# Expert gathers of a two-layer decoder trunk: v rows follow their u rows by one head instead of by a pair of heads

## Chip, cores, metric

One core of one Trainium2 chip runs one launch of the kernel, all in float32. The metric is the device time in microseconds (us) of that launch. It is the median of three runs.

## What is computed

The reference is a decoder trunk of two layers over one sequence of 256 tokens with 1024 channels. Layer 0 mixes tokens with gated linear attention, layer 1 with a gated DeltaNet. Behind each mixer stands a PEER channel mixer, and this is where the change is made. Every token has 8 heads. Each head picks 16 of 16,384 experts by product keys, and an expert is one row of `u` and one row of `v`, each of 1024 floats (4 KB):

```python
def peer_ffn(h, wq, k1, k2, u, v):
    ...
    v1, i1 = lax.top_k(s1, PEER_TOPK)
    v2, i2 = lax.top_k(s2, PEER_TOPK)
    ...
    sc, pos = lax.top_k(cand, PEER_TOPK)
    idx = jnp.take_along_axis(cand_idx, pos, axis=-1)
    gate = jax.nn.softmax(sc, axis=-1).astype(h.dtype)
    ...
    def block(args):
        tb, ib, gb = args
        ue = jnp.take(u, ib, axis=0)
        act = gb * jax.nn.gelu(jnp.einsum('nd,nkd->nk', tb, ue))
        ve = jnp.take(v, ib, axis=0)
        return jnp.einsum('nk,nkd->nd', act, ve)
```

So for each of 256 tokens, 128 rows of u and 128 rows of v are fetched in each of two layers. The order is fixed by the data: a head's v rows can be fetched as soon as its indices are known, but they can be weighted only after all 16 dots of that head are done.

## The kernel before

The function `decoder` interleaves the PEER mixers with the rest of layer 1. It runs four stages w = 0 to 3: layer 0 on tokens 0 to 127, layer 0 on tokens 128 to 255, then layer 1 on the same two blocks. Next to stages 1 and 2 runs the DeltaNet mixer of token block 0 and of block 1 (I call it the mixer). It has a ramp of projections (`gdn_qkv`), a core of chunked products, the projections `gdn_z` and `gdn_w_out`, and the queries and scores of layer 1's experts (`peer_wq`). Stage w+1 of layer 1 can't choose experts before that. The mixer of block 1 starts from the residual that stage 1 writes (L1144 to L1148).

A stage has 128 u gathers and 128 v gathers. A gather is one indirect DMA that POOL (GpSimd) issues: 128 rows of 4 KB, one to each partition.

- **u gathers** (L2025) bring slot s of all 128 tokens into one of 8 buffers `ub`. DVE (VectorE) multiplies the buffer with h and sums it into one column of `dots` (L1163).
- **v gathers** (L2038) bring, for each of four groups of 32 tokens, rows of several tokens by several slots, so that PE (TensorE) can sum them in PSUM with a 128 x 32 matrix of weights `z` (L1652, 8 matmuls for a set of four gathers). They use 12 buffers (9 of `vb`, 3 of `mods`). In the last phase of a stage every second set goes into `ub`.

Before the change all this is done by pairs of heads, 32 slots at a time. A stage has five phases (`phase`): u of pair 0 alone; u of pair p with v of pair p-1, one after the other, three times; v of pair 3 alone. A v gather has four tokens by 32 slots, and a pair has 8 sets.

At the end of a pair comes a chain over four engines: the last dot (DVE), gelu (ACT, ScalarE, L1353), gate times dots and a spread by `mask4` (`weights`, L1116 and L1117), a transpose (PE, L1621), and the copy into `z` (ACT, L1360). The indices take a similar way: `routing` (DVE, L1028 to L1090), a transpose (L1631) and `slot_rows` (L1106 to L1109) into `idx4`, from which the v gathers read. `routing(k)` picks the experts of pair k; `idx_ready` tells POOL that its u gathers may start. The first v gather of stage 0 also waits for `cols_summed`, which PE gives after L1713, since `vb` holds partial sums until then.

Each engine's program is a set of generators (`experts`, `mixer`) whose pieces carry due times; `interleave` sorts the pieces by these. The order is thus fixed when the kernel is built, and an engine runs it strictly in order. Due times of the expert side come from `phase`, from `turned_in` and `routed_in` (which slot a routing or transpose stands behind) and from `ROUTE_AT`. `landings` works out which buffer each gather uses and whom POOL waits for. Two details matter: a u gather n waits for dot n-8 (or, behind a stage's end, for the v set that used the buffer), and the first v set that uses `ub` in the last phase waits for all dots of the stage.

The routings of stages 2 and 3 begin only when the scores are there. In the last phase of stages 1 and 2, DVE runs three of them (pairs 0, 1, 2 of the next stage) and only then the residual (L1144 to L1148) and the next stage's dots; pair 3 is routed from slot 42 of the next stage.

## Time and profile before

| | |
|---|---|
| runs of the kernel before, us | 1881.61, 1894.21, 1881.12 (median 1881.61) |
| profiled execution, us | 1885.82 |
| its span, first to last instruction, us | 1884.0 |
| PE, DVE, ACT, POOL busy, share of the span | 76%, 64%, 21%, 58% |
| bytes moved, mean rate | 703.24 MB, 373 GB/s |
| indirect gathers | 512 of u, 512 of v |
| dots L1163 | 512, mean 1.22 us |

The profile is of one execution. An engine's timeline gives the start of a piece, its length and, in brackets, how long the engine sat idle before it and what ended this. Stretches (windows) give busy time of each engine, the granted PE clock as a share of full speed, the DMA share and the rate in GB/s. Times are counted from the first instruction.

### The profile page before, as it was taken

Reading aid. Unit: us, or ns where it says so; the run is one execution under the profiler, and the core shown is the slowest. Engines: PE = TensorE matmul, PEld = TensorE weight load, DVE = VectorE, ACT = ScalarE, POOL = GpSimd, SP = SyncE. Lnnn points to the kernel's source line nnn. Section 1 sums busy time; section 2 is a strip of 40 time slices with the busy share of each in tenths; the row PEclk is TensorE's granted clock in tenths of the full one; section 3 lists DMA queues with packets and bytes.
Section 4 is the critical chain, followed back from the end, with each engine's and each line's share of the span. In section 5 each row is a group of like instructions: output and inputs, shape, how many; then the busy total and the mean of one; then the engine's idle time right before and its main releaser. Section 6 shows DMA issues by size and latency. Waiting matters only on the chain.

```text
span 1884.0 us, 20383 instructions
## 1 busy us (share of the span) xinstructions
PE 1440.3 (76%) x7476; PEld 868.7 (46%) x7476; DVE 1206.4 (64%) x2707; ACT 387.9 (21%) x910; POOL 1088.5 (58%) x1067
## 2 busy tenths in 40 slices
PE   6989896756668758979898777897988862767567
PEld 6744696200011647757665376776756620101011
DVE  6588468788881677576443967867733498754440
ACT  1202110000000561451202265163221120000000
POOL 0111047777777566666653557576665357777754
PEclk8989995787779879989998877998989885676789
DMA  9989289999999999999999999899999999999997
GB/s 367 371 337 354 100 324 318 410 409 409 406 374 401 359 408 345 347 410 402 363 414 412 376 378 408 297 365 410 355 401 415 409 346 395 409 409 409 409 399 298
DMA packets 173972, 703.24 MB, mean 373 GB/s; under 512 B 23456, under 2 KB 23840, under 8 KB 155824
## 3 DMA queue, kind: packets, MB, share of 16 engines
q0 software_dynamic: 152640, 574.69, 78.5%
q1 hardware_dynamic: 21232, 127.25, 16.9%
q8 instruction: 59, 0.97, 0.2%
q14 instruction: 41, 0.34, 0.0%
HBM read 700.82 MB, written 1.05 MB: 373 GB/s over the span
## 4 chain that ended last, share of the span: by engine, by line
POOL 25%; PE 20%; DMA 20%; DVE 12%; issue 10%; ACT 3%; POOLq 0%; DVEq 0%; ACTq 0%
POOL ub L2025 12%; DMA ub<-in_peer_u,idx 11%; POOL vb L2038 9%; DMA vb<-in_peer_v,idx 5%; DVE ub L1163 5%; PE PS L1652 4%; PE PS L1699 3%; POOL mods L2038 3%; PE PS L1942 2%; POOL ub L2038 2%; PE PS L1863 2%; DMA ub<-in_peer_v,idx 2%; PE PS L1858 1%; PE PS L1845 1%; DVE ring L1282 1%
## 5 line engine op out<-in xcount | busy, mean ns | idle before, releaser
L2025 POOL DMA_INDIRECT ub<-in_peer_u,idx x512 | 541.7, 1058 | 339.4 <-DVE dots L1163 158.2
L1163 DVE CUSTOM_DVE_ANT_0 ub<-ub,h 128x1024 f32<-128x1024 f32 x384 | 464.3, 1222 | 225.3 <-DMA ub<-in_peer_u,idx 223.4
L1652 PE MATMUL PS<-vb,z 128*32 128x512 f32 x1348 | 407.7, 751 | 125.3 <-DMA vb<-in_peer_v,idx 122.0
L2038 POOL DMA_INDIRECT vb<-in_peer_v,idx x337 | 352.4, 1046 | 127.7 <-issue 99.1
L1652 PEld LDWEIGHTS PS<-vb,z 128*32 128x32 f32 x1348 | 66.0, 122 | 368.6 <-DMA vb<-in_peer_v,idx 271.2
L1163 DVE CUSTOM_DVE_ANT_0 ub<-ub,PS 128x1024 f32<-128x1024 f32 x128 | 154.2, 1220 | 111.0 <-DMA ub<-in_peer_u,idx 111.0
L1652 PE MATMUL PS<-mods,z 128*32 128x512 f32 x444 | 144.3, 754 | 56.1 <-DMA mods<-in_peer_v,idx 56.1
L2038 POOL DMA_INDIRECT mods<-in_peer_v,idx x111 | 114.5, 1032 | 33.8 <-issue 33.8
L1768 PE MATMUL PS<-hT,ring 128*128 128x128 f32 x1024 | 125.4, 285 | 2.9 <-DMA ring<-in_gdn_qkv 2.9
L1768 PEld LDWEIGHTS PS<-hT,ring 128*128 128x128 f32 x1024 | 122.5, 201 | 10.3 <-issue 6.7
L2038 POOL DMA_INDIRECT ub<-in_peer_v,idx x64 | 60.0, 937 | 83.8 <-DVE dots L1163 57.2
L1652 PEld LDWEIGHTS PS<-mods,z 128*32 128x32 f32 x444 | 23.4, 123 | 142.8 <-DMA mods<-in_peer_v,idx 120.4
L424 POOL DMA_DIRECT2D two_slots<-in_ada_wide x24 | 12.9, 537 | 125.2 <-DVE vb L664 57.4
L1652 PE MATMUL PS<-ub,z 128*32 128x512 f32 x256 | 68.7, 626 | 11.6 <-DMA ub<-in_peer_v,idx 11.6
L1463 ACT ACTIVATE ring<-ring,taps 128x128 f32<-128x128 f32 x256 | 76.4, 387 | 0.3
L1353 ACT ACTIVATE dots<-dots 128x32 f32<-128x32 f32 x16 | 3.7, 229 | 316.8 <-DVE dots L1163 316.8
L1942 PE MATMUL PS<-ring,hT 128*128 128x256 f32 x256 | 61.0, 399 | 5.8 <-ACT z L1360 3.8
L1991 PEld LDWEIGHTS PS<-hT,ring 128*128 128x128 f32 x512 | 60.8, 199 | 7.2 <-issue 5.0
L1961 PE MATMUL PS<-ring 128*128 128x256 f32 x256 | 60.6, 397 | 4.6 <-DMA ring<-in_gdn_w_out 4.6
L1991 PE MATMUL PS<-hT,ring 128*128 128x128 f32 x512 | 62.4, 283 | 1.5 <-ACT z L1360 1.5
L1699 PE MATMUL PS<-hT,ring 128*128 128x256 f32 x256 | 58.0, 387 | 1.2 <-DVE zero L1121 1.2
L1942 PEld LDWEIGHTS PS<-ring,hT 128*128 128x128 f32 x256 | 50.2, 199 | 18.2 <-ACT z L1360 4.5
(351 smaller groups left out, 2194.6 us busy)
## 6 DMA issues: line engine op xcount, KB each, us to landing
ring<-in_gdn_qkv SPq DMA_DIRECT2D x32, 1024.0 KB, 8.6
two_slots<-in_ada_wide POOLq DMA_DIRECT2D x24, 1024.0 KB, 10.1
ring<-in_peer_wq SPq DMA_DIRECT2D x24, 1024.0 KB, 8.0
ring<-in_gdn_z SPq DMA_DIRECT2D x16, 1024.0 KB, 8.7
ring<-in_gdn_w_out SPq DMA_DIRECT2D x16, 1024.0 KB, 8.6
ring<-in_gla_w_in SPq DMA_DIRECT2D x6, 2048.0 KB, 12.0
mods<-in_ada_wide POOLq DMA_DIRECT2D x12, 1024.0 KB, 7.7
ring<-in_ada_w SPq DMA_DIRECT2D x4, 2048.0 KB, 11.6
```

What stands on the lines that cost most here:

```text
L1163: dve.tensor_tensor_reduce(out=ub[:, n % UB, :], in0=ub[:, n % UB, :], in1=by_token, scale=1.0, scalar=0.0, op0=ALU.mult, op1=ALU.add, acc ...
L1282: dve.tensor_tensor(dst[:, vs, :], dst[:, vs, :], core.ps(name, lv, gq), ALU.add).then_inc(emptied["D"].sem, 1)
L1463: last = act.activation(tapped_by[:, j, c, :], here[:, c, j:j + P], ACT.Copy, scale=taps[:, j, 16 * hf + 4 * un + c:16 * hf + 4 * un + c + 1])
L1652: last = pe.matmul(y[32 * j:32 * j + 32, e, :], z[:, j, 28 * b:28 * b + 32], rows[:, e * 512:(e + 1) * 512], start=False, stop=False, skip ...
L1699: last = pe.matmul(PS[:, 3 + b % 2, c * S:(c + 1) * S], w[:, k, c * P:(c + 1) * P], hT[:, k, :], start=(k == 0), stop=(k == KD - 1))
L1768: last = pe.matmul(PS[:, 3 + un, (2 * bb + c) * P:(2 * bb + c + 1) * P], w[:, k, c * P:(c + 1) * P], hTm[:, k, :], start=(k == 0), stop=(k ...
L1863: last = pe.matmul(ps[:, e, :], Y[:, v_, :], XT[:, v_, :], start=True, stop=True)
L1942: last = pe.matmul(ps, hTm[:, k, :], w[:, k, :], start=(k == 0), stop=(k == KD - 1))
L1961: last = pe.matmul(ps, oT[:, part * KD + k, :], w[:, k, :], start=(part == k == 0), stop=(part == 1 and k == KD - 1))
L1991: last = pe.matmul(PS[:, 3 + un % 2, (2 * bb + c) * P:(2 * bb + c + 1) * P], w[:, k, c * P:(c + 1) * P], hTm[:, k, :], start=(k == 0), sto ...
L2025: pool.indirect_dma_start(ub[:, n % UB, :], None, u_rows, off).then_inc(u_land[n % UB].sem, 16)
L2038: pool.indirect_dma_start(rows, None, v_rows, off).then_inc(land.sem, 16)
```

## The change

The lag between u and v becomes one head. A stage has nine phases: u of head 0 alone (16 slots), u of head p with v of head p-1 (seven times 16 pairs of gathers), v of head 7 alone. A v gather has eight tokens by 16 slots, a head has 4 sets, and `z` is half as large. Gelu, weights, transpose and the copy into `z` are made per head, 32 times instead of 16, on tiles of 16 columns (the spread tile stays 128 x 128, by `mask8`). Routing stays by pairs; its index tile is spread in two parts and turned by two transposes, and `slot_rows` becomes one reduction and one copy. The last phase has 16 v gathers instead of 32, and DVE routes two pairs there instead of three. Pair 2 of stages 2 and 3 is now routed from slot 12 on in the next stage, pair 3 from slot 40 on. The number of gathers, dots and v matmuls doesn't change.

```diff
-            def turned_in(w, p):
...
-            def routed_in(w, p):
...
+            def routed_in(w):
+
+                k = w * PAIRS
                 if w == 0:
-                    return [[(0, 3, 8), (1, 20, 24)], [(2, 20, 24)], [(4, 3, 8), (3, 20, 24)], [(5, 3, 8), (6, 20, 24)]][p]
...
+                    return [(1, 7), (2, 32), (4, 48), (3, 64), (5, 80), (6, 96), (7, 112)]
+                return [] if w == 1 else [(k + 2, 12), (k + 3, 40)]
...
-                return W_AT[w] + scale * (0, 60, 152, 244, 336)[p], scale * (60, 92, 92, 92, 46)[p]
+                return W_AT[w] + scale * (30 + 47 * (p - 1) if p else 0), scale * (30 if p == 0 else 23 if p == HEADS else 47)
...
-                        pairs = turned_idx.rearrange("p (n a) -> p n a", a=2)
-                        link(dve.tensor_copy(half4, pairs[:, :, 0]))
-                        link(dve.tensor_tensor(half4, half4, pairs[:, :, 1], ALU.add))
-                        quads = half4.rearrange("p (n a) -> p n a", a=2)
-                        dve.tensor_tensor(idx4[:, k % IDX4, :], quads[:, :, 0], quads[:, :, 1], ALU.add).then_inc(rows_ready.sem, 1)
...
+                        link(dve.tensor_reduce(rows_f[:], turned_idx.rearrange("p (n a) -> p n a", a=8), AX, ALU.add))
+                        dve.tensor_copy(idx4[:, k % IDX4, :], rows_f[:]).then_inc(rows_ready.sem, 1)
...
+                        link(dve.tensor_tensor(mine, dots[:, q % 2, :], mine, ALU.mult))
+                        dve.tensor_tensor(spread_a[:], mine.unsqueeze(1).to_broadcast([P, 8, TOPK]), mask8[:], ALU.mult).then_inc(acts_ready.sem, 1)
...
-                                        for n in range(3):
-                                            yield ROUTE_AT[w + 1] + 12 * n
-                                            for i, _ in enumerate(routing(k + n)):
-                                                yield ROUTE_AT[w + 1] + 12 * n + 0.75 * i + 1
+                                        for n in range(2):
+                                            yield ROUTE_AT[w + 1] + 18 * n
+                                            for i, _ in enumerate(routing((w + 1) * PAIRS + n)):
+                                                yield ROUTE_AT[w + 1] + 18 * n + i + 1
...
-                                                last = pe.matmul(y[32 * j:32 * j + 32, e, :], z[:, j, 28 * b:28 * b + 32],
...
+                                            last = pe.matmul(y[32 * j:32 * j + 32, e, :], z[:, j, 24 * b:24 * b + 32],
```

How the order moves is seen at three places. First POOL at the start of stage 0. Before:

```order
L2010 IOTA iota 128x16
L2025 DMA ub<-in_peer_u,idx 128x1024 x33
L2038 DMA vb<-in_peer_v,idx 128x1024
L2025 DMA ub<-in_peer_u,idx 128x1024
L2038 DMA vb<-in_peer_v,idx 128x1024
```

and after:

```order
L2012 IOTA iota 128x16
L2028 DMA ub<-in_peer_u,idx 128x1024 x17
L2043 DMA vb<-in_peer_v,idx 128x1024
L2028 DMA ub<-in_peer_u,idx 128x1024
L2043 DMA vb<-in_peer_v,idx 128x1024
```

The first v gather stands behind 17 u gathers instead of 33.

Second, PE in the ramp of stage 1: the last projections of the mixer (L1768, after: L1770) and the start of its core (L1795, after: L1797). L1621 (after: L1625) is the transpose of the weights, L1652 (after: L1657) a v set. Before:

```order
L1768 MATMUL PS<-hT,ring 128x128 x64
L1751 MATMUL PS<-ones,ring 128x1 x8
L1758 MATMUL PS<-ident,inv 128x128 x8
L1768 MATMUL PS<-hT,ring 128x128 x32
L1795 MATMUL PS<-tri,g 128x128 x4
L1621 MATMUL PS<-ident,spread_a 128x128
```

and after:

```order
L1625 MATMUL PS<-ident,spread_a 128x128
L1607 MATMUL PS<-ones,zero 128x512 x2
L1770 MATMUL PS<-hT,ring 128x128 x16
L1657 MATMUL PS<-vb,z 32x512 x8
L1770 MATMUL PS<-hT,ring 128x128 x16
L1753 MATMUL PS<-ones,ring 128x1 x8
L1760 MATMUL PS<-ident,inv 128x128 x8
L1770 MATMUL PS<-hT,ring 128x128 x16
L1657 MATMUL PS<-vb,z 32x512 x8
L1770 MATMUL PS<-hT,ring 128x128 x16
```

The first weights of the stage are now turned in the middle of the ramp, and v sets stand between its projections; before, none stood there.

Third, DVE in the ramp of stage 2 after the change. L1081 to L1087 are the three longest steps of `routing` for pair 2 of that stage, L1168 the dots, L1227 to L1231 the mixer:

```order
L1227 TENSOR_TENSOR ring<-ring 128x512
L1168 ISA ub,dots<-ub,h 128x1024
L1168 ISA dots 128x1
L1081 TENSOR_TENSOR fold<-cand,iota 128x1024
L1230 TENSOR_TENSOR ring<-ring 128x512
L1231 TENSOR_TENSOR ring<-ring 128x512
L1240 TENSOR_TENSOR be<-be,beta 128x16
L1168 ISA ub,dots<-ub,h 128x1024
L1168 ISA dots 128x1
L1085 TENSOR_TENSOR fold<-fold,topf 128x1024
L1168 ISA ub,dots<-ub,h 128x1024
L1168 ISA dots 128x1
```

The same place before had the dots and the mixer alone:

```order
L1214 TENSOR_TENSOR hT<-hT,PS 128x512
L1222 TENSOR_TENSOR ring<-ring 128x512
L1163 ISA ub,dots<-ub,h 128x1024
L1163 ISA dots 128x1
L1225 TENSOR_TENSOR ring<-ring 128x512
L1226 TENSOR_TENSOR ring<-ring 128x512
L1235 TENSOR_TENSOR be<-be,beta 128x16
L1163 ISA ub,dots<-ub,h 128x1024
L1163 ISA dots 128x1
```

A routing that stood behind the last dot of stage 1 now stands among the first dots of stage 2.

## Rows read from the trace of the kernel before

**Rows 1.** The page: span and rate.

```profile
span 1884.0 us, 20383 instructions
...
HBM read 700.82 MB, written 1.05 MB: 373 GB/s over the span
```

**Rows 2.** Stretches: PE, PEld, DVE, ACT, POOL busy, PEclk, DMA share, GB/s.

```profile
246.00:312.00 66.00, 61.48 (x324) 58.19 (x322) 49.12 (x130) 8.70 (x19) 40.21 (x33) 0.76 0.91 328
...
1060.00:1100.00 40.00, 30.88 (x149) 18.98 (x150) 34.11 (x101) 11.66 (x23) 22.77 (x20) 0.72 0.91 330
...
1540.00:1577.00 37.00, 0.90 (x2) 0.36 (x2) 36.38 (x76) 4.24 (x6) 24.47 (x26) 0.50 0.95 351
1584.00:1813.00 229.00, 150.24 (x361) 23.94 (x362) 126.57 (x254) 4.32 (x9) 172.87 (x185) 0.71 1.03 409
```

**Rows 3.** Timelines of PE, DVE and POOL at the start of stage 0.

```profile
276.59 16.97 PE L1713 MATMUL PS<-ones,vb 128*128 128x1 f32 x96
...
276.79 0.22 DVE L1106 COPY fold<-PS 128x64 f32<-128x64 f32 x1 [4.78 <-PE PS L1631]
...
312.31 1.09 POOL L2038 DMA_INDIRECT vb<-in_peer_v,idx  x1 [0.30 <-issue]
```

**Rows 4.** Issues of L2025 (u): 296 to 312, then 1540 to 1577.

```profile
L2025 POOL DMA_INDIRECT ub<-in_peer_u,idx x9: 933/1461/1988, 296.3 to 311.1; - x9
...
L2025 POOL DMA_INDIRECT ub<-in_peer_u,idx x26: 932/937/1836, 1539.2 to 1575.9; - x26
```

**Rows 5.** Timelines at the end of stage 1; 16th v gather of the last pair.

```profile
1018.17 1.23 DVE L1163 CUSTOM_DVE_ANT_0 ub<-ub,h 128x1024 f32<-128x1024 f32 x1 [4.42 <-DMA ub<-in_peer_u,idx]
...
1028.29 0.88 DVE L1028 MAX8 top<-mods 128x8 f32<-128x128 f32 x4 [8.06 <-ACT mods L1573]
...
L2038 POOL DMA_INDIRECT ub<-in_peer_v,idx x2: 937/938/940, 1032.1 to 1033.3; - x2
...
DMA to landing us min/median/max: 13.5/13.6/13.6
...
1066.68 0.94 POOL L2025 DMA_INDIRECT ub<-in_peer_u,idx  x1 [7.28 <-PE PS L1652]
...
1074.76 0.29 DVE L1090 TENSOR_TENSOR spread_i<-idxf,mask 128x128 f32<-128x128 f32 x1
...
1075.81 1.12 PE L1607 MATMUL PS<-ones,zero 128*128 128x512 f32 x2
...
1078.31 1.22 DVE L1163 CUSTOM_DVE_ANT_0 ub<-ub,h 128x1024 f32<-128x1024 f32 x1
```

**Rows 6.** The same at the end of stage 2.

```profile
L2038 POOL DMA_INDIRECT ub<-in_peer_v,idx x1: 938/938/938, 1500.6 to 1500.6; - x1
...
DMA to landing us min/median/max: 11.5/11.5/11.5
...
1525.08 0.93 POOL L2025 DMA_INDIRECT ub<-in_peer_u,idx  x1 [0.31 <-issue]
...
1542.79 1.21 DVE L1163 CUSTOM_DVE_ANT_0 ub<-ub,PS 128x1024 f32<-128x1024 f32 x1
...
1544.28 0.94 POOL L2025 DMA_INDIRECT ub<-in_peer_u,idx  x1 [2.89 <-DVE dots L1163]
1545.52 1.84 POOL L2025 DMA_INDIRECT ub<-in_peer_u,idx  x1 [0.30 <-DVE dots L1163]
```

**Rows 7.** Timelines of ACT and PE in the ramp of stage 1.

```profile
655.71 1.28 ACT L1469 ACT_TABLE_LOAD   x1
657.00 0.22 ACT L1469 ACTIVATE be<-gc 128x16 f32<-128x16 f32 x1
...
689.50 1.28 ACT L1353 ACT_TABLE_LOAD   x1
...
692.34 0.63 ACT L1440 ACTIVATE vT<-ring 128x512 f32<-128x512 f32 x1
...
692.56 0.47 PE L1621 MATMUL PS<-ident,spread_a 128*128 128x128 f32 x1 [7.84 <-DVE spread_a L1117]
```

More of the change, by code:

```diff
@@ L1149, in experts @@
                                     break
-                                ahead = [(routing(j), j, first) for j, first in routed_in(w, p)]
-                                late = {5: [k] if k == 0 else [k, k + 1], 12: [k + 2] if k else []} if w != 1 and p == 0 else {}
                                 if layer and p == 0:
@@ L1362, in experts @@
[L1362 to L1368 removed]
+                                    act.activation(z[:].rearrange("p j (b m) -> p j b m", m=4 * 8)[:, :, :, 0:8],
+                                                   turned_act.rearrange("p (j b a) -> p j b a", j=4, a=8), ACT.Copy).then_inc(z_made.sem, 1)
```

231 lines of the change are left out of this document (116 added, 115 removed).

## The prediction

> **What bounds the kernel now.** I read the page first: 700.82 MB are read in a span of 1884.0 us, 373 GB/s on average [rows 1]. Then the stretches. Where u and v gathers alternate and nothing else asks for the DMA, it runs at 409 GB/s for 229 us without a break [rows 2]. A gather is 128 x 4096 bytes = 524,288 bytes, so it takes 1.28 us there. At that rate the 700.82 MB would take 1713 us. The kernel is therefore bound by DMA, plus some 170 us in which the DMA runs below its rate. The change leaves every byte in place, so it can only move time in and out of those 170 us.
>
> The reader should look for them at the seams of the four stages: 328 GB/s in the first 66 us of stage 0, 330 GB/s between stages 1 and 2, 351 GB/s at the start of stage 3 [rows 2]. In the last two, DVE is busy for 34.1 of 40 us and 36.4 of 37 us: the seams belong to DVE. Last come the timelines around each seam [rows 3, 5 to 7]; they say which wait ends last.
>
> **The change, part by part.** The sum is made against the profiled execution, 1885.8 us, that is the span of 1884.0 us and 1.8 us around it. It lies 4.2 us above the median of the runs, 1881.6 us.
>
> *Steady phases.* Gathers, dots and v matmuls are the same in number and size. In the long stretch DVE is busy 126.6 of 229 us and PE 150.2 [rows 2]. The 16 added ends of a head (gelu, a weights step of 0.2 + 0.3 us like the spread of 0.29 us in [rows 5], a transpose, a copy into z) are about 1.3 us of work each, spread over four engines. They hide under the DMA. The chain also has time: a head's first v set lands four u and four v gathers behind the head's last dot, some 10 us by 1.28 us. Cost 0. If that cover were gone, 16 chains of about 5 us would be 80 us; nothing in the stretch points that way.
>
> *Start of stage 0.* One would hope that v gathers fill the 66 us at 328 GB/s, which lack (1 - 328/409) x 66 = 13 us. They can't do so early. The first v gather needs `cols_summed`, and PE gives it at 276.6 + 17.0 = 293.6 us [rows 3], behind projections that the change doesn't move. POOL runs in order. After the change it has issued 17 u gathers by about 280 (the last needs dot 8, which stands behind the index rows that DVE makes at 276.8), then stands until 293.6. From there u and v alternate at 1.28 us: the 34th gather goes out at 293.6 + 16 x 1.28 = 314. Before, the 33rd and 34th go out at 311.1 and 312.3 [rows 3, 4]. So the hoped-for gain is eaten by a wait that is late next: cost 1 to 2 us, I take +1, bounds -4 (POOL's issues are shorter, see below) and +5.
>
> *Ramp of stage 1.* Here two effects meet. Before, PE sits 7.8 us in front of the transpose of the first weights, and on ACT the gelu with its two table loads takes from 689.5 to 692.3, right on the way to the core [rows 7]. Both move into the middle of the ramp, where ACT and PE have pauses: a gain of up to 2.8 us. Against this, PE must now take three v sets before the core starts. The last of these twelve v gathers is the 40th gather of the stage, against some 34 before, and six gathers are 6 x 1.28 = 8 us of DMA; most of it is paid by two 1 MB weight blocks that are fetched later (2 x 2 x 1.28 = 5 us). Besides, the lists of instructions have 4 more table loads in stage 1 and 6 more in stage 2, at 1.28 us each: 5 and 8 us of ACT. ACT is idle for most of the span, so I charge a third to the path. Net for stage 1: -2.8 + 3 + 1.7 = +2, bounds -4 and +8. Of this I take +1.
>
> The row shows what a table load costs: it starts at 655.71, lasts 1.28 us, and the next activation starts at 657.00, 0.01 us behind it [rows 7]. The Trainium skill, ScalarE: Activation LUTs, section "What ACT_TABLE_LOAD costs", adds a drain of about 1.38 us to each load, 2.66 us in all. By that rule the ten loads would be 27 us of ACT instead of 13. The trace disagrees with the drain here.
>
> *Seam of stages 1 and 2.* This is the largest term. Before, the last dot ends at 1019.4, the scores arrive at 1028.3, and three routings run from 1028.3 to 1075.0, 15.6 us each; y closes at 1076.9, and the first dot of stage 2 starts at 1078.3 [rows 5]. So the three routings just fit under the 32 last v gathers. After the change only 16 v gathers are left when the last dot is done. The DMA is saturated, so the place in its queue decides: the last u row lands where before the 16th v gather of the last pair landed, at 1033.3 + 13.6 = 1046.9 [rows 5]. The last dot then ends at 1048.3 instead of 1019.4. Two routings of 15.8 us (each has one more spread of 0.29 us) and the weights step take DVE to 1048.3 + 0.8 + 31.6 = 1080.7. The residual takes 1078.3 - 1075.0 = 3.3 us. The first dot of stage 2 starts at 1084.0: +5.7 us. The new wait is y, closed at 1076.9, waiting for DVE. Behind it are queued the mixer of block 1, which reads the residual, and all dots, and behind the dots POOL, whose ninth u gather needs a dot. The u indices themselves are ready at 1049.1 + 15.8 = 1065, against an issue at 1066.7 [rows 5]; they just don't bind. Charge +5.5, bounds +1 (last dot earlier) and +11 (last dot at 1054, if the last 12 v gathers, which wait for it, end no earlier than now).
>
> *Ramp of stage 2.* The third routing, 15.5 us of DVE, moves in among the first 28 dots. In its favour, six fewer dots stand before the core, 7.4 us. Net 8 us more DVE work in about 75 us, in which DVE waits now and then. But DVE runs in order, and the 1.2 us steps stand between the mixer's own. I take half: +4, with the table loads and the effects of stage 1, bounds 0 and +10.
>
> *Seam of stages 2 and 3.* Same working. The 16th v gather of the last pair lands at 1500.6 + 11.5 = 1512.1 [rows 6]; the last dot ends at 1513.4, routings at 1545.8, residual at 1549.1, against a first dot at 1542.8: +6.3 us. Here the DMA decides alone. Nine dots at 1.24 us later, at 1560.2, POOL may issue the 17th u gather, and from then on v gathers fill in at 1.28 us: the 33rd gather goes out at 1560.2 + 16 x 1.28 = 1580.7. Before, the 32nd went out at 1575.9 [rows 4], the 33rd 1.24 us later at 1577.1. That is +3.5. Charge +3, bounds +1 and +7. The fourth routing is spread over slots 12 to 27: 1.1 us a step with a dot of 1.2 us, under 2.56 us for two gathers. No cost.
>
> *End.* 28 v gathers behind the last dot become 12, with the same last landing. Cost 0.
>
> **Sum.** 1 + 1 + 5.5 + 4 + 3 = 14.5 us. 1885.8 + 14.5 = 1900.3 against the profiled execution, and 1881.6 + 14.5 = 1896 against the median.
>
> **Rivals.**
>
> A, faster: the one-sided stretches are what starves the DMA, and the change halves them. The mechanism is POOL's issue time. In stage 0, while dots read `ub` and h from SBUF back to back, an issue of a u gather takes a median of 1.46 us and up to 1.99; in stage 3, where h lies in PSUM, it takes 0.94 [rows 4]. With the 0.3 us between issues, 1.76 us is more than the DMA's 1.28. When v gathers alternate, DVE works half as densely and the issues should shrink. The Trainium skill, SBUF — State Buffer, section on the two sides of SBUF, gives the cause: DVE and GpSimd share one port pair under an exclusive lock, and a DVE operation with two SBUF inputs takes it. By that rule the trace agrees in stages 0 and 3. The price: the three seams of [rows 2] lack 13 us, (1 - 330/409) x 40 = 8 us and (1 - 351/409) x 37 = 5 us, together 26 us. Half of it would give 1869, all of it 1856; I take 16 us, 1866. It decides if the first dot of stage 2 isn't later than about 1079. Against it stands that two of the three seams end in a wait for DVE, which grows.
>
> B, clearly slower: the head's chain doesn't hide in stages 1 and 2. PE waited 7.8 us for one such chain in the ramp [rows 7]. The eight added ones could cost PE 1 to 2 us each, and the v sets in the ramp hold the core back by their full 8 us: the sum plus 10 to 15 us, 1906 to 1911.
>
> C, nothing: routing two pairs instead of three cancels against the later last dot, because stages 1 and 2 are bound by the DMA in their second half and catch up. 1882, within 4 us. For it speaks that the DMA's queue is deep when the last dot ends, 13.5 us from issue to landing [rows 5]: there the DMA sets the pace.
>
> D, the change doesn't do what it says at the start: it is part of the sum, since v gathers don't start before 293.6.
>
> **How the numbers follow.** A measurement tells about 1% from no change, 18.8 us: 1862.8 and 1900.4. Chances: forecast 0.42, of which 0.31 within 1% and 0.11 beyond; A 0.22, its 16 us being just under 1%: 0.12 beyond, 0.10 within; B 0.22, all beyond; C 0.14, all within. Faster 0.12, same 0.55, slower 0.33. The bounds of the terms add up to -6 and +41; that all fall on one side is rare, so the forecast's own range is 1886 to 1908. The whole range reaches down to A's 1866 and up to B's 1911: 1865 to 1912.
>
> **What would show it.** Right: the first dot of stage 2 comes 5 to 6 us later measured from y's closing, with DVE busy and no idle before the residual; the first v gather is issued at 293.6 behind a wait for PE; the stretch of stage 3 stays at 409 GB/s. Wrong: DVE idle before the residual at both seams (then A or C), or idle time of PE in front of the transposes in stages 1 and 2 that sums to over 20 us (B).

## The result and the profile after

The changed kernel takes 1917.9 us (median of four runs, 1915.7 to 1921.9), the kernel before 1882.1 in the same comparison: a ratio of 1.0177 (95% interval 1.0149 to 1.0204). It is slower by 1.8%. The forecast was 1896 with a range up to 1912, so the result lies outside. The two profiled executions below differ by 30.1 of these 35.8 us. One remark on all runs: ratios and their intervals leave out executions in a slower state of the chip, the medians of the experiments don't, so the two can differ (most in run 11).

The page of the changed kernel, its span beside 1884.0 in [rows 1]:

```profile
span 1914.1 us, 20618 instructions
...
PE 1443.3 (75%) x7508; PEld 856.0 (45%) x7508; DVE 1215.1 (63%) x2739; ACT 420.9 (22%) x961; POOL 1078.3 (56%) x1067
```

Over the span as a whole no engine is near its limit, and the long stretch of stage 3 stays at 409 GB/s, as in [rows 2]. The time went into the other places. Stretches of the changed kernel, columns as in [rows 2]: the first 20 us in which v gathers could have helped, then stage 1 cut at the mixer's two cores (ramp, core 1, between them, core 2), then the rest:

```profile
280.00:300.00 20.00, 10.76 (x48) 10.16 (x49) 16.94 (x52) 2.17 (x4) 8.34 (x7) 0.50 0.37 114
...
624.10:703.10 79.00, 54.50 (x369) 43.76 (x369) 44.56 (x84) 45.25 (x114) 56.95 (x51) 0.81 0.99 386
703.10:775.20 72.10, 61.85 (x483) 51.79 (x483) 51.74 (x95) 21.61 (x54) 37.72 (x38) 0.95 0.94 343
775.20:834.90 59.70, 48.89 (x379) 38.00 (x379) 32.54 (x61) 32.49 (x93) 41.12 (x38) 0.92 1.00 396
834.90:908.80 73.90, 64.26 (x498) 52.98 (x499) 53.31 (x98) 22.84 (x56) 41.32 (x41) 0.95 0.97 365
...
1600.00:1840.00 240.00, 150.29 (x388) 24.05 (x388) 146.06 (x315) 8.33 (x17) 181.40 (x193) 0.74 1.03 409
```

The same of the kernel before (start, ramp, core 1, between, core 2):

```profile
280.00:300.00 20.00, 18.63 (x92) 18.54 (x91) 19.59 (x47) 1.51 (x2) 11.18 (x10) 0.51 0.76 230
...
620.00:683.70 63.70, 43.85 (x317) 42.70 (x318) 43.53 (x83) 37.37 (x91) 38.48 (x34) 0.79 0.99 382
683.70:766.10 82.40, 66.29 (x504) 52.47 (x502) 59.13 (x108) 28.56 (x74) 53.62 (x52) 0.94 0.96 365
766.10:820.40 54.30, 48.80 (x378) 38.66 (x378) 30.96 (x57) 31.45 (x85) 40.55 (x38) 0.94 0.94 367
820.40:896.10 75.70, 63.50 (x498) 51.54 (x497) 55.46 (x100) 21.56 (x58) 46.84 (x43) 0.93 1.02 404
```

The reader is to see two things. The ramp grew from 63.7 to 79.0 us, with DMA full in both: the core starts late because more gathers are served ahead of it. To serve them takes transfer time and also PE's own time. PE is busy in the ramp for 10.7 us more (54.5 for 43.9) and idle for 4.6 us more, and the matmuls of v sets, of which there were none before, are 9.3 us of it (the ramp, L1657 alone; PE and PEld busy, PEclk, DMA share, GB/s):

```profile
624.10:703.10 79.00, 9.29 (x48) 1.68 (x48) 0.81 0.99 386
```

The edits of phase 0 to the changed kernel below move the transfers and PE's work on them together, so their shares aren't told apart on this side. The second thing: DMA time lost, (1 - rate/409) x length, moved: core 1 loses 8.9 us before and 11.6 after, the piece between 5.6 and 1.9, core 2 0.9 and 8.0. With the other pieces of the stage the loss grows by 6.5 us, about the stage's extra length (6.8). The end of the mixer is hardly late: its last scores are out 434.6 us behind the stage's first dot, before 432.6 (stage 2: 442.0 and 439.6). What is late is the last dot, 433.7 us behind the first instead of 399.4.

Cut by y's closing and by the first dots, the two profiled executions differ by 30.1 us (all in us):

| part | before | after | difference |
|---|---|---|---|
| to the first u gather | 246.0 | 241.8 | -4.2 |
| stage 0, from there to y's closing | 372.7 | 380.9 | +8.2 |
| stage 1, first dot to y's closing | 456.9 | 463.7 | +6.8 |
| y's closing to first dot of stage 2 | 1.4 | 7.2 | +5.8 |
| stage 2 | 458.5 | 464.9 | +6.4 |
| y's closing to first dot of stage 3 | 6.0 | 14.0 | +8.0 |
| stage 3 | 333.7 | 332.8 | -0.9 |

(The seam between stages 0 and 1 has 1.4 in both.) The -4.2 is not the change's: over all profiles of this study the first u gather comes at 241 to 250 us, with either lag.

PE ahead of the two cores of stage 1, after the change (timeline; L1797 is the core's first piece):

```profile
664.71 0.47 PE L1625 MATMUL PS<-ident,spread_a 128*128 128x128 f32 x1 [9.65 <-DVE spread_a L1123]
...
694.72 1.04 PE L1657 MATMUL PS<-mods,z 128*32 128x512 f32 x2 [2.12 <-DMA mods<-in_peer_v,idx]
699.75 1.06 PE L1657 MATMUL PS<-mods,z 128*32 128x512 f32 x1 [3.99 <-DMA mods<-in_peer_v,idx]
703.14 1.05 PE L1797 MATMUL PS<-tri,g 128*128 128x128 f32 x7
...
834.01 0.47 PE L1625 MATMUL PS<-ident,spread_a 128*128 128x128 f32 x1 [5.41 <-DVE spread_a L1123]
```

Ahead of core 1 stand a head's transpose (9.65 us of waiting) and three v sets; right ahead of core 2 stands another head's transpose (5.41). None of the three v sets stood there before. Over the whole kernel PE's wait for `spread_a` went from 63.0 us in 10 pieces to this (waits):

```profile
PE PS L1625 <- DVE spread_a L1123: 97.8, 27, 16.8
```

In stages 1 and 2 alone it more than doubled (waits from 620 to 1543 us before, then from 624 to 1574 after):

```profile
PE PS L1621 <- DVE spread_a L1117: 17.9, 4, 7.8
```

```profile
PE PS L1625 <- DVE spread_a L1123: 40.4, 13, 9.6
```

The seam of stages 1 and 2, DVE after the change (timeline), to be held against [rows 5]:

```profile
1056.56 1.23 DVE L1168 CUSTOM_DVE_ANT_0 ub<-ub,h 128x1024 f32<-128x1024 f32 x1 [1.50 <-DMA ub<-in_peer_u,idx]
...
1075.82 0.19 DVE L1091 TENSOR_TENSOR idx<-cand 128x32 uint32<-128x32 f32 x1
...
1091.51 0.19 DVE L1091 TENSOR_TENSOR idx<-cand 128x32 uint32<-128x32 f32 x1
...
1092.25 0.68 DVE L1151 TENSOR_TENSOR h<-PS,h 128x512 f32<-128x512 f32 x1
...
1094.91 1.22 DVE L1168 CUSTOM_DVE_ANT_0 ub<-ub,h 128x1024 f32<-128x1024 f32 x1
```

y closed at 1087.7 (PE, L1610). The residual carries no wait in brackets: it comes straight behind the second routing. And POOL at the start of stage 0 (timeline), against [rows 3, 4]:

```profile
275.66 0.94 POOL L2028 DMA_INDIRECT ub<-in_peer_u,idx  x1 [10.90 <-DVE dots L1168]
289.83 0.94 POOL L2043 DMA_INDIRECT vb<-in_peer_v,idx  x1 [13.24 <-PE PS L1715]
291.07 1.62 POOL L2028 DMA_INDIRECT ub<-in_peer_u,idx  x1 [0.30 <-issue]
292.99 1.87 POOL L2043 DMA_INDIRECT vb<-in_peer_v,idx  x1 [0.30 <-issue]
```

### The profile page after: what moved, and what is told of

It is laid out like the page before. It is cut to its first block, busy times and chain, and to the rows that moved or that the text cites. A ratio compares the mean times of both kernels' runs of the same rounds, so it can differ in the third digit from the quotient of the medians.

```text
span 1914.1 us, 20618 instructions
## 1 busy us (share of the span) xinstructions
PE 1443.3 (75%) x7508; PEld 856.0 (45%) x7508; DVE 1215.1 (63%) x2739; ACT 420.9 (22%) x961; POOL 1078.3 (56%) x1067
## 4 chain that ended last, share of the span: by engine, by line
POOL 26%; PE 22%; DMA 15%; DVE 12%; issue 11%; ACT 3%; POOLq 0%; ACTq 0%; DVEq 0%
POOL ub L2028 13%; POOL vb L2043 9%; DMA ub<-in_peer_u,idx 9%; DVE ub L1168 4%; PE PS L1657 4%; POOL mods L2043 3%; DMA mods<-in_peer_v,idx 3%; PE PS L1701 3%; PE PS L1993 2%; PE PS L1847 1%; PE PS L1865 1%; PE PS L1860 1%; DVE ring L1287 1%; DMA ring<-in_peer_wq 1%; DMA ring<-in_gdn_z 1%
## 5 line engine op out<-in xcount | busy, mean ns | idle before, releaser
L1168 DVE CUSTOM_DVE_ANT_0 ub<-ub,h 128x1024 f32<-128x1024 f32 x384 | 465.2, 1222 | 266.2 <-DMA ub<-in_peer_u,idx 264.3
L1657 PE MATMUL PS<-vb,z 128*32 128x512 f32 x1440 | 433.8, 761 | 134.0 <-DMA vb<-in_peer_v,idx 121.1
L2043 POOL DMA_INDIRECT vb<-in_peer_v,idx x360 | 369.8, 1027 | 155.2 <-issue 107.0
L1657 PEld LDWEIGHTS PS<-vb,z 128*32 128x32 f32 x1440 | 68.4, 122 | 382.7 <-DMA vb<-in_peer_v,idx 268.5
L1657 PE MATMUL PS<-mods,z 128*32 128x512 f32 x480 | 170.0, 772 | 77.6 <-DMA mods<-in_peer_v,idx 77.6
L1168 DVE CUSTOM_DVE_ANT_0 ub<-ub,PS 128x1024 f32<-128x1024 f32 x128 | 155.4, 1220 | 114.0 <-DMA ub<-in_peer_u,idx 113.7
L2043 POOL DMA_INDIRECT mods<-in_peer_v,idx x120 | 120.3, 1003 | 36.6 <-issue 36.6
L1770 PEld LDWEIGHTS PS<-hT,ring 128*128 128x128 f32 x1024 | 124.8, 203 | 10.6 <-issue 8.8
L1770 PE MATMUL PS<-hT,ring 128*128 128x128 f32 x1024 | 127.2, 287 | 1.4 <-DMA ring<-in_gdn_qkv 1.4
L1657 PEld LDWEIGHTS PS<-mods,z 128*32 128x32 f32 x480 | 27.0, 123 | 182.1 <-DMA mods<-in_peer_v,idx 154.5
L1358 ACT ACTIVATE dots<-dots 128x16 f32<-128x16 f32 x32 | 6.9, 216 | 456.8 <-DVE dots L1168 456.2
L1625 PE MATMUL PS<-ident,spread_a 128*128 128x128 f32 x32 | 12.4, 387 | 97.8 <-DVE spread_a L1123 97.8
L1625 PEld LDWEIGHTS PS<-ident,spread_a 128*128 128x128 f32 x32 | 5.0, 158 | 128.2 <-DVE spread_a L1123 124.9
L1287 DVE TENSOR_TENSOR ring<-ring,PS 128x512 f32<-128x512 f32 x72 | 46.5, 683 | 22.0 <-PE PS L1865 22.0
L2043 POOL DMA_INDIRECT ub<-in_peer_v,idx x32 | 30.2, 945 | 48.4 <-DVE dots L1168 39.6
## 6 DMA issues: line engine op xcount, KB each, us to landing
ring<-in_gla_w_in SPq DMA_DIRECT2D x6, 2048.0 KB, 10.8
```

The source lines that it names most:

```text
L1168: dve.tensor_tensor_reduce(out=ub[:, n % UB, :], in0=ub[:, n % UB, :], in1=by_token, scale=1.0, scalar=0.0, op0=ALU.mult, op1=ALU.add, acc ...
L1287: dve.tensor_tensor(dst[:, vs, :], dst[:, vs, :], core.ps(name, lv, gq), ALU.add).then_inc(emptied["D"].sem, 1)
L1657: last = pe.matmul(y[32 * j:32 * j + 32, e, :], z[:, j, 24 * b:24 * b + 32], rows[:, e * 512:(e + 1) * 512], start=False, stop=False, skip ...
L1770: last = pe.matmul(PS[:, 3 + un, (2 * bb + c) * P:(2 * bb + c + 1) * P], w[:, k, c * P:(c + 1) * P], hTm[:, k, :], start=(k == 0), stop=(k ...
L2043: pool.indirect_dma_start(rows, None, v_rows, off).then_inc(land.sem, 16)
```

## The experiments

They ran on five other chips, one for each group below (1 to 4, 5 to 8, 9 to 12, 13 to 16, 17 and 18), on which the kernel before takes 1985 to 2005 us and spreads by 1% and more. In the undisturbed part of stage 3 such a chip moves 366 GB/s (1700 to 1800 us of run 1) where the first moved 409. Times are therefore held only against runs of the same group. The last four columns are from one profiled execution each: stage 0 from its first u gather to y's closing; from the first dot of stage 1 to that of stage 2, and from there to stage 3's, so stage and seam together; stage 3 to y's closing; and the sum from stage 1 on. Stage 0 jumps between 397 and 410 us without any edit (runs 5, 6, 13, 17 and 18 have the same stage 0), so the last column is the better one for edits in stages 1 to 3.

| run | kernel | median, us | ratio to before (95%) | stage 0 | stages 1, 2 with seams | stage 3 | 1 to 3 |
|---|---|---|---|---|---|---|---|
| 1 | after, phase 0 of 60 | 2026.4 | 1.0110 (1.0074 to 1.0145) | 404.7 | 496.5, 501.2 | 364.8 | 1362.5 |
| 2 | after, residual first | 2005.5 | 1.0012 (0.9972 to 1.0052) | 406.4 | 485.1, 496.3 | 371.6 | 1353.0 |
| 3 | after, sums early | 2035.5 | 1.0137 (1.0052 to 1.0222) | 417.3 | 488.1, 516.7 | 362.2 | 1367.0 |
| 4 | before, two routings | 2014.4 | 1.0036 (0.9995 to 1.0076) | 397.9 | 487.8, 495.4 | 372.9 | 1356.1 |
| 5 | after | 2010.4 | 1.0146 (1.0101 to 1.0191) | 407.2 | 489.9, 495.5 | 362.0 | 1347.4 |
| 6 | after, residual first | 2000.6 | 1.0064 (1.0033 to 1.0096) | 397.5 | 481.3, 496.7 | 375.1 | 1353.1 |
| 7 | after, phase 0 of 45 | 1992.4 | 1.0016 (0.9981 to 1.0051) | 407.2 | 483.0, 486.6 | 359.9 | 1329.5 |
| 8 | after, slack | 2069.5 | 1.0428 (1.0386 to 1.0470) | 400.5 | 531.2, 528.3 | 358.9 | 1418.4 |
| 9 | after, 6 and 7 together | 1991.1 | 0.9997 (0.9962 to 1.0032) | 406.7 | 483.0, 481.9 | 367.8 | 1332.7 |
| 10 | before, residual first | 2016.3 | 1.0114 (1.0048 to 1.0180) | 402.5 | 480.8, 491.9 | 382.1 | 1354.8 |
| 11 | after, no gelu | 2014.7 | 1.0070 (1.0017 to 1.0123) | 398.7 | 489.8, 490.2 | 361.3 | 1341.3 |
| 12 | before, no gelu | 1981.5 | 1.0002 (0.9962 to 1.0042) | 397.9 | 482.4, 478.8 | 361.1 | 1322.3 |
| 13 | after | 2026.4 | 1.0120 (1.0065 to 1.0176) | 409.5 | 497.9, 505.0 | 362.0 | 1364.9 |
| 14 | after, start later | 2016.2 | 1.0073 (1.0039 to 1.0107) | 404.1 | 498.2, 501.9 | 361.8 | 1361.9 |
| 15 | before, phase 0 of 45 | 2020.2 | 1.0098 (1.0062 to 1.0133) | 398.1 | 494.8, 510.7 | 363.1 | 1368.6 |
| 16 | after, 6, 7 and 14 together | 1989.4 | 0.9960 (0.9928 to 0.9991) | 398.7 | 480.5, 478.9 | 370.5 | 1329.9 |
| 17 | after, no gelu | 2011.3 | 1.0135 (1.0082 to 1.0188) | 407.0 | 485.3, 499.4 | 361.7 | 1346.4 |
| 18 | after | 2011.0 | 1.0109 (1.0055 to 1.0164) | 400.2 | 490.3, 506.0 | 361.9 | 1358.2 |

**The change itself (5, 13).**

> The changed kernel as it is, a control: the first four experiments ran on a chip where the kernel before takes 2004.6 us instead of 1882, so they lack a partner. Expected: the ratio of the first comparison, 1.0177 (1.0149 to 1.0204), within its interval on any chip if the loss is made of fixed waits; less, say 1.010, on a chip whose DMA is slower, since waits of DVE and PE then hide under it.

> The changed kernel again, as the partner of the next three on their chip. Expected 1.0146 to 1.0177 times the kernel before.

1.0146, 1.0120 and 1.0109 (run 18), each with an interval of 0.5%: the loss is there on the slower chips too. It looks a little smaller, but the intervals overlap with that of 1.0177.

**What stands ahead of the mixer's core (1, 7, 15, 8).**

```diff
 def phase(w, p):
+    first = 45 if w in (1, 2) else 30        # 60 in run 1
+    each = (A - 23 - first) / (HEADS - 1)
-    return W_AT[w] + scale * (30 + 47 * (p - 1) if p else 0), scale * (30 if p == 0 else 23 if p == HEADS else 47)
+    return W_AT[w] + scale * (first + each * (p - 1) if p else 0), scale * (first if p == 0 else 23 if p == HEADS else each)
```

> The changed kernel, but in stages 1 and 2 phase 0 of the expert side gets due times of 60 units instead of 30, so that PE's first v sets and the first heads' weight transposes stand behind the start of the mixer's core, as in the kernel before. Theory P (v sets and head chains in PE's row hold the mixer back): the first core starts some 10 us earlier in the stage (after: 79 and 77 us behind the stage's first dot; before: 64 and 65), the second core too, and stages 1 and 2 from first dot to y's closing lose most of their 6.7 and 6.4 us: 1918 falls to about 1907. Theory S (the stages' extra time is made at their ends, where the last 12 v gathers wait for all dots, or by DVE's routings): the core starts earlier, but the stages' lengths and the time stay within 3 us of 1918.

> The changed kernel with phase 0 of stages 1 and 2 at 45 units, half way to experiment 1: one or two of the three v sets and one head's chain move behind the start of the mixer's core. Theory P: the core starts some 5 us earlier in its stage, and the time falls by 3 to 8 us. Theory S: within 3 us of the changed kernel. If phase 0 of 60 units had made things worse by starving the DMA in the ramp, this one shows half of it.

With 45, one v set and 22 dots stand ahead of core 1 instead of three and 27; the core of stage 1 starts 60.5 us behind the stage's first dot instead of 76.2 (run 5). Both stages with their seams get 6.9 and 8.9 us shorter, the kernel 18 us by the medians (0.9%) and 1.3% by the ratios. On this chip the gain goes through the mixer's end: its last scores are out 446.5 and 446.8 us behind the stage's first dot instead of 453.9 and 454.8. With 60, no v set and 16 dots stand there, the core starts after 53.1 us, and most of the gain is gone (1.0110, on a chip on which the changed kernel itself wasn't run): core 1 then has to carry the gathers. Its stretch, first of run 1 (706 to 800 us), then of run 7 (715 to 800):

```profile
706.00:800.00 94.00, 71.32 (x503) 57.87 (x502) 58.30 (x110) 30.32 (x77) 54.67 (x51) 0.87 0.85 304
```

```profile
715.00:800.00 85.00, 67.81 (x503) 55.98 (x500) 56.53 (x102) 26.32 (x69) 52.12 (x48) 0.90 0.93 345
```

At 304 GB/s DMA loses 24 us in it, at 345 GB/s 13. The second core goes the other way (14 us in run 1, 20 in run 7), and over the first 475 us of stage 1 the difference is 7 us. So both too many and too few gathers ahead of the core cost.

What else did the edit repair? PE's wait for `spread_a` stays as it was over the kernel (86.9 us in 19 pieces, 83.4 in 15 in run 5) and over stages 1 and 2 (19.8 and 18.8). But it stands elsewhere. Between a stage's first dot and its second core PE idles in front of the heads' transposes for 6.2 us (stage 1) and 16.4 us (stage 2) in run 5, and for 1.2 and 2.7 in run 7. Run 7 alone therefore doesn't separate the gathers ahead of the cores from the chains ahead of them. Run 15 does, since it hardly has such waits.

The reverse, on the kernel before: `starts = (0, 45, 142, 239, 336, 382) if w in (1, 2)` in place of `(0, 60, 152, 244, 336)`.

> The kernel before (lag of a pair) with phase 0 of stages 1 and 2 at 45 units instead of 60: the reverse of experiment 7. By the due times 39 dots and one v set then stand in front of the mixer's first core instead of 30 dots and none. Theory P (how many gathers stand in front of the core decides, not the lag itself): the core starts some 10 us later in its stage, ratio 1.005 to 1.012. If it is the head's chain that matters (PE in front of a transpose), which is not changed here: 0.998 to 1.003.

37 dots and one v set stand ahead of its core, 41 gathers where the change has 40. The core starts 85.7 us behind the first dot (64.3 in run 12, on another chip, the kernel before without gelu). It is 1.0% slower than the kernel before, though its lag is a pair, its chains and routings stand at the same slots, and PE waits for `spread_a` for only 1.2 us in stages 1 and 2. PE's matmuls of v sets ahead of its core are 1.9 us only. So such an order costs 1.0% by itself; a shorter lag and waits for a chain aren't needed for it. The changed kernel costs 1.2% on this chip. That the same mechanism makes up most of that is inferred, not measured.

```diff
-    yield t0 + (1.2 if p == HEADS else span * 2.2 / TOPK)
+    late = 3 if w in (1, 2) and p < HEADS - 1 else 0
+    yield t0 + (1.2 if p == HEADS else span * (2.2 + late) / TOPK)
...
-    yield t0 + span * (4 * b + 4) / TOPK
+    yield t0 + span * (4 * b + 4 + (late if p else 0)) / TOPK
```

> The changed kernel with the transposes of weights, the copies into z and the v sets of heads 0 to 5 of stages 1 and 2 due three slots later in PE's and ACT's order. Theory P in its first half (PE stands in front of a head's transpose: 9.65 us ahead of core 1 and 5.41 us ahead of core 2 in the trace after): these waits fall under 1 us, the waits of PE for spread_a over the kernel fall from 97.8 us to under 60, and the time falls by 5 to 10 us. If the v sets' landing is what holds the core and the chain only waits beside it: within 3 us; if later v sets free the v buffers too late and POOL stands: slower.

The last clause came true, and far beyond its size: 59 us slower than run 5. Waits of POOL, run 8 and below it run 5:

```profile
POOL vb L2044 <- PE PS L1658: 289.3, 46, 18.0
```

```profile
POOL vb L2043 <- PE PS L1657: 49.9, 9, 17.2
```

Twelve v buffers are three sets, and a head has four. Sets that PE takes three slots later free them too late, and POOL, which issues in order, stops u with v. PE's wait for `spread_a` fell a little (78.9 us, 10 times, for 83.4, 15 times), but POOL's stop covers whatever that was worth, so this run doesn't price the chain.

**What stands ahead of the residual (2, 6, 4, 10).** Pair 1 is routed in the next stage:

```diff
-    return [] if w == 1 else [(k + 2, 12), (k + 3, 40)]
+    return [] if w == 1 else [(k + 1, 2), (k + 2, 20), (k + 3, 40)]
...
-    for n in range(2):
+    for n in range(1):
         yield ROUTE_AT[w + 1] + 18 * n
```

> The changed kernel with only one routing (pair 0) between the last dot and the residual at the ends of stages 1 and 2; pair 1 is routed from slot 2 of the next stage, pair 2 from slot 20. Theory D (DVE's routings stand in front of the residual and the first dots): between y's closing and the next stage's first dot there were 7.2 us and 14.0 us after the change, against 1.4 and 6.0 before; both fall to about 1.5 to 6, so 6 + 8 = 14 us less, of which the moved routing costs up to 5 in the next ramp: 1918 falls to 1904 to 1909. Theory N (the seam is bound by DMA landings and the routing moves its 15.8 us unchanged into the ramp, where DVE is short too): 1915 to 1921.

> The same kernel as in experiment 2 (one routing ahead of the residual), beside the changed kernel on the same chip. Theory D: 10 to 14 us below the changed kernel (0.5 to 0.75%). Theory N: within 3 us of it.

Run 2 is at 1.0012, run 6 at 1.0064, each on its own chip. The residual now waits for y, as in the kernel before (timeline of DVE, run 6):

```profile
1118.64 0.69 DVE L1151 TENSOR_TENSOR h<-PS,h 128x512 f32<-128x512 f32 x1 [1.81 <-PE PS L1607]
```

The seams are 1.5 and 4.9 us instead of 21.4 and 15.9 in run 5. That is 31 us, and the stages give all of it back: y closes 11 us later in stage 1, 12 in stage 2, and stage 3 takes 13 us more (375.1 for 362.0). From stage 1 on run 6 takes 1353.1 us and run 5 1347.4. The routings are DVE's work of 15.6 us each, and in these two profiles it is paid for wherever it stands. The medians do differ by 10 us (1.0064 against 1.0146, intervals apart), but in the two profiles the only part that got shorter is stage 0 (9.7 us), which the edit doesn't touch; where the medians' difference comes from stays open. The seams on these chips are also longer than the 7.2 and 14.0 of the first. One more wait has a part in it, in run 5 (DVE, then ACT):

```profile
1107.40 0.17 DVE L1122 TENSOR_TENSOR gate<-dots,gate 128x16 f32<-128x16 f32 x1 [22.27 <-ACT dots L1358]
```

```profile
1102.43 0.60 ACT L1581 ACTIVATE ring<-PS 128x512 f32<-128x512 f32 x1 [18.19 <-remote]
...
1105.86 1.28 ACT L1358 ACT_TABLE_LOAD   x1
1107.15 0.21 ACT L1358 ACTIVATE dots<-dots 128x16 f32<-128x16 f32 x1
```

The gelu of the last head stands on ACT behind the mixer's query copies (L1581), which are late there; behind it stand both routings. On the first chip the same wait was 2.5 us. Not all of the lateness is the kernel's order: PE's last projection ends at 1092.7, and the copy starts at 1102.4, behind a wait whose end the profile lays to nothing in this kernel (`remote`). Nor are seam and ramp independent. In run 7, whose routings stand where run 5's do, DVE waits 0.3 us here, since the last dot comes 448.3 us behind the first instead of 433.2, and the seams are 4.0 and 12.5 us.

> The kernel before with one part of the change alone: two routings instead of three at the ends of stages 1 and 2, pair 2 routed from slot 12 of the next stage. If the moved routing is a cost of its own in the ramp (my term of 4 us at most): seams shorten (the last two routings end 15 us earlier, so y's closing ends them: first dot of stage 3 4 us earlier), ramp of stage 2 longer by up to 8: total 1878 to 1886. If the ramp hides it: 1876 to 1880. If DVE's steps hold up the mixer fully: 1890 or more.

1.0036 (0.9995 to 1.0076), not to be told apart from no change; at most 0.8%. Both seams are at 1.4 us, and stage 3 takes 372.9 us where the other runs of its group but run 2 take 362 to 365: gained at the seam, given back behind it.

> The kernel before (lag of a pair) with one routing instead of three ahead of the residual, pair 1 routed from slot 2 and pair 2 from slot 16 of the next stage. The seam of before is closed by y, not by DVE (first dot 1.4 us behind y in stage 2, 6.0 in stage 3), so at most 5 us are to be had at the second seam, and the moved routings cost in the ramp: ratio 0.998 to 1.005. If routings ahead of the residual cost as much before as after: 0.992.

1.0114: worse than both guesses. Against run 12 (without gelu) its seams gain 3.7 and 2.9 us, but stage 2 with its seam is 13 us longer (491.9 for 478.8), and two routings more in stage 3 cost that stage 21 us (382.1 for 361.1). So in the kernel before the routings ahead of the residual were well placed.

**The start (3, 14).** In run 3 the column sums stand ahead of PE's last two projections. In run 14 POOL alone is changed: in phase 1 of stage 0, v gather s stands behind u gather s + 8.

```diff
+    back = 8 if w == 0 and p == 1 else 0
-    for s in range(TOPK):
+    for s in range(TOPK + back):
...
+        s -= back
-        if p:
+        if p and s >= 0:
```

> The changed kernel with PE's 48 column sums put ahead of the last two projections of stage 0, so that the first v gather doesn't wait for them. Theory W (the wait for the column sums starved the DMA at the start): the first v gather is issued near 277 instead of 289.8, the stretch 280 to 300 moves well over its 114 GB/s, and the time falls by 6 to 10 us. Theory M (the last two projections and the scores get late by 17 us and hold up the next routing or the mod blocks; or the u gathers alone couldn't fill the DMA anyway): within 3 us of 1918 or slower.

> The changed kernel; in phase 1 of stage 0 alone POOL issues the v gathers of head 0 eight slots later, so that u gathers and not a wait stand in its row until the column sums are there. Theory W (the wait for the column sums costs 4 us at the start): the stretch from 280 to 300 us moves more than the 114 GB/s of the changed kernel (before: 248 in the same place), stage 0 gets 3 to 5 us shorter, ratio about 0.2% below the control. If u gathers can't go either because their dots stand behind DVE's index rows: no difference in the stretch and in the time (within 2 us).

Run 3 went as theory M has it. The transpose of the first index rows stands behind those projections, so DVE stood for 28.64 us at L1113, and POOL with it (timeline of POOL, run 3):

```profile
300.61 0.94 POOL L2028 DMA_INDIRECT ub<-in_peer_u,idx  x1 [29.55 <-DVE dots L1168]
```

Stage 0 takes 417.3 us, 11 us more than in any other run of its group. Run 14 went as theory W has it. The stretch from 280 to 300 us, run 14, then run 13:

```profile
280.00:300.00 20.00, 12.17 (x52) 11.12 (x52) 19.59 (x58) 2.88 (x4) 9.49 (x10) 0.50 0.73 229
```

```profile
280.00:300.00 20.00, 11.54 (x51) 10.91 (x51) 17.37 (x54) 2.46 (x4) 7.85 (x7) 0.50 0.33 109
```

(The 248 GB/s that the expectation gives for the kernel before belong to 286 to 306 us; from 280 to 300 it is 230.) The 34th gather goes out 64.8 us behind the first instead of 71.2, and the last of the stage is still 5.3 us earlier; stage 0 is 5.4 us shorter. That is less than stage 0 jumps by itself. The medians differ by 10 us, more than the start explains, and the intervals of the two ratios (1.0073 and 1.0120) overlap slightly. So the earlier gathers are shown, their worth in time only roughly.

**Gelu's table loads (11, 12, 17, 18).** `ACT.Gelu_apprx_tanh` becomes `ACT.Copy`; gelu is left out.

> The changed kernel with a plain copy in place of gelu (gelu is left out), so that a head's end needs no load of ACT's gelu table: fewer of the 88 table loads, and a chain shorter by up to 2.6 us (two loads of 1.28 us, before and behind). With its partner, the same edit of the kernel before. If the table loads carry the loss (a third of 13 us in my sum): the ratio of after to before without gelu falls from 1.0146 or more to 1.010 or less. If the order of PE carries it: the ratio stays at 1.013 to 1.018.

> The kernel before with a plain copy in place of gelu (gelu is left out), the partner of the one above. Expected within 4 us of the kernel before, since its 16 chains hide; the 7.8 us that PE waits for one in the ramp of stage 1 lose 2.8 us at most.

> The changed kernel with a plain copy in place of gelu (gelu is left out), as in experiment 11, now beside the changed kernel itself on one chip. If the added table loads carry a part of the loss (experiment 11 gave a ratio of 1.007, within 0.5%, against 1.0146 and 1.012 for the changed kernel on other chips): 0.5 to 0.8% below its partner. If they hide, as two thirds of them did in my sum: within 0.3% of it.

> The changed kernel, the partner of the one above: 1.012 to 1.0177 times the kernel before.

Run 11 alone looked as if the loads were half of the loss (1.0070; by the medians of all executions it is 1.3%, 2014.7 for 1989.1). Beside its own partner nothing is left in the medians: 2011.3 against 2011.0. ACT is busy for 369.2 us in run 17 and 421.8 in run 18, with 48 table loads for 88. So 40 loads and 53 us of ACT show no cost, but the two ratios, each within 0.5%, still allow some 0.5%, or 10 us. The profiles don't help: from stage 1 on run 17 is 11.8 us shorter (1346.4 for 1358.2), in stage 0 6.8 us longer.

**All repairs together (9, 16).**

> The changed kernel with both repairs: phase 0 of stages 1 and 2 at 45 units (experiment 7: 1.3% below the changed kernel on its chip) and one routing ahead of the residual (experiment 6: 0.8% below it). If the two causes are independent (ramp and seam), the gains add: 2.1% below the changed kernel, a ratio to the kernel before of about 0.993 to 0.997. If they are one cause (both merely let the mixer start earlier), the ratio stays at 1.000 to 1.003.

> The changed kernel with the later start (experiment 14), phase 0 at 45 units and one routing ahead of the residual. If the start's repair is worth 4 us beside the other two: a ratio of 0.996 to 0.999, the first below the kernel before. If not: 1.000 as in experiment 9.

Run 9 is at 0.9997 (0.9962 to 1.0032), next to the guess of one cause; its interval just reaches into the other. Run 16 is at 0.9960, with an interval that ends at 0.9991: faster than the kernel before by 0.4%, and by 1.6% than the changed kernel beside it (37 us by the medians, with a spread of some 10). Its seams are all 1.4 us and its first cores start after 60.4 and 60.3 us. From stage 1 on it takes 35 us less than run 13 (1329.9 for 1364.9). But run 7, on its chip, takes 1329.5 without the residual's edit, and run 9 1332.7 with it: across chips, the last column shows no gain of that edit beside the first. Stage 3's 370.5 us are what the moved routings cost. A kernel with the 45 units and the later start alone would be the next to measure; it wasn't run.

## Why the prediction failed

*Right were the direction and what happens at the first seam. Wrong were the terms for the start, for the ramps with the cores behind them, and for the second seam.* Point by point:

**Steady phases, cost 0.** Right for stage 3: 409 GB/s, and -0.9 us for the stage. But the sentence "They hide under the DMA" was meant for all stages and was read from a stretch without a mixer. In stages 1 and 2 the second core had no term at all, and there DMA lost 7.1 and 5.5 us more than before (stage 1: 0.9 to 8.0).

**Start, +1.** The 34th gather was forecast for 314 and came at 314.8. It was held against 312.3 on the same clock, though, and the start is to be counted from the first u gather: 66.3 us before, 73.0 after, so +6.7, beyond my bound of +5. The wait was where I had put it (13.24 us in front of the first v gather); its price was not 1. That the clock time fitted is luck: the wait ended at 289.8 instead of 293.6, and the 16 gathers behind it took 25.0 us instead of 20.5. Run 14 gets 6.4 us back at the 34th gather. The rest of stage 0's +8.2 is in the last phase, which no run touched.

**Ramp of stage 1, +1 (bounds -4 and +8).** With the next step, the one that failed most. I counted "the 40th gather of the stage, against some 34 before". What the runs speak for is what is served, dots and v sets, before the core's first piece: 30 gathers before (30 dots), 40 after (28 dots and three sets). I charged half of 6 gathers' DMA time and nothing for PE's own work on the sets (9.3 us), and subtracted 2.8 us for the chain. That gain couldn't come: the transpose of [rows 7] stands at 692.56, inside the core that had begun at 683.7, and now PE waits 9.65 us for one ahead of the core. The core came 15.4 us later. It isn't all lost, since a later core holds fewer gathers (72.1 us long for 82.4), but then DMA starves in the cores. Stage 1 cost +6.8, stage 2 +6.4, where the sum had +1 and, for stage 2, +4 mostly for the routing. Runs 7 and 15 show on other chips, from both sides, that the order ahead of the core is worth 1%; on the first chip its share is argued from the profiles. That table loads would take "a third to the path" isn't settled: run 17 shows no cost, but can't exclude these 4 us. The Trainium skill (ScalarE: Activation LUTs, "What ACT_TABLE_LOAD costs") adds a drain of about 1.38 us to each load; run 5 again shows none, with a load of 1.28 us at 1105.86 and the next activation at 1107.15.

**Seam of stages 1 and 2, +5.5.** Right in place and size: +5.8 from y's closing, with DVE busy through. Runs 6 and 9 add what I had not seen: this wait is DVE's work and not idleness, and where it was moved, the stages that then carry it took in the profiles what the seam gave. The routings took 31.5 us for my 31.6. The last dot came at 1057.8, not 1048.3, but y, which I had left at 1076.9, closed 10.8 us later as well, so the difference stood. The size is to that extent luck: the first dot came at 1094.9 for a forecast 1084.0.

**Seam of stages 2 and 3, +3.** Under-sized: +8.0. I had worked out +6.3 for the first dot and then let "the DMA alone" decide by the 33rd gather. DMA decided nothing there: both routings stood ahead of the residual as in the first seam, and the 33rd gather of stage 3 went out 47.7 us behind y's closing instead of 40.3.

**Ramp of stage 2, +4.** Not told apart from the core's order. Run 4, with an interval from -0.05% to +0.76%, allows -1 to +15 us for the moved routing.

**The rivals.** B came nearest, and its own sign came true: PE's idle time in front of the transposes in stages 1 and 2 is 40.4 us (17.9 before), where I had named 20. B had two halves. "The v sets in the ramp hold the core back" is what runs 7, 1 and 15 support. "The head's chain doesn't hide" is open on the first chip, where these waits grew by 22.5 us and no run removed them. On the others it isn't needed: run 5 has 18.8 us of them and is still 1.5% slower, and run 15 loses 1.0% with 1.2 us. Its 1906 to 1911 was still too low, since the start and the second seam were as short in it as in my sum. A had its mechanism half right. The issues of u gathers did not shrink (median 1.48 us from 295 to 314 us, for 1.46 in [rows 4]), but the v issues between them take 0.94 us in the median, and from the first v gather on a gather goes out every 1.56 us. The wait ahead of it ate that gain. The Trainium skill's rule on the lock of DVE and GpSimd (SBUF — State Buffer, on the two sides of SBUF) fits the long issues of u gathers there, but nothing in the time hung on it. C fell with both stages, which did not catch up.

Terms that the profiles put in place of mine, on the first chip (together 30.1): start +6.7, ramps and cores about +13 (6.8 and 6.4), seams +13.8, the rest of stage 0 +1.5, stage 3 -0.9, less 4.2 for a start that moves by itself.

Where these parts lie is measured on the first chip; that losses of their size can be taken back at the start and the ramps is shown on others, and no experiment ran on a chip of the first kind. Open besides: what share of the gain of run 16 is the residual's edit, whose medians (0.8% in run 6) and profile disagree; and the end of stage 0, where POOL stands for all dots in front of the first v set that uses `ub`, for which no kernel was run.

## What to carry to other kernels

Where one engine's program interleaves a latency-bound chain with a stream of transfers, count what the program serves ahead of the chain's first piece, in served items and not in issued ones, and compare that count before and after. A change of granularity moves the due times of everything tied to it; set them anew (here one number, 30 to 45, was worth 1.3% by the ratios) before judging the change. A seam in which an engine works without idling wasn't repaired here by moving its work: look first at who would carry it instead.

## What the hardware showed that I had not expected

- The same program moved 409 GB/s through a stretch of alternating gathers on the first chip (DMA share 1.03) and 366 on another (1700 to 1800 us of run 1, DMA share 0.97). The four other chips of the later runs were like it in time (run 5: 367 GB/s from 1740 to 1840 us). In the end of stage 1, with weight blocks among the gathers, run 7 reached 410 GB/s (988 to 1131 us). Why the gathers alone are slower there stays open.
- On the five slower chips each profile has 37 to 58 pieces of idle time, 214 to 331 us in sum over the engines, whose end it lays to no work of the kernel (`remote`); the two profiles of the first chip have none. What ends them, and whether they are the chips' difference, stays open.
- The shorter waits of one chip can hide a wait that is long on another: DVE waited 2.5 us for the last head's gelu on the first chip and 22.3 us in run 5, in the same program.
- 53 us of ACT's work, forty table loads among them, could be taken out without a change in the median (2011.3 for 2011.0 us, each ratio within 0.5%).
